# The last feed-forward chunk in halves of features, the next step's first transposes inside its last block, and the next weight piece converted in halves, its low half by GpSimd

## The reference

```python
def _rmsnorm(x, g):
    y = x * lax.rsqrt(jnp.mean(x * x, axis=-1, keepdims=True) + EPS)
    return y * g
def _swiglu(x, wg, wu, wd):                  # wg, wu: 1024 x 2816, wd: 2816 x 1024
    return (jax.nn.silu(x @ wg) * (x @ wu)) @ wd
# first block, per layer: feed-forward, mixer, feed-forward, each between two norms
h = _swiglu(_rmsnorm(x, g[0]), ...);  x = x + 0.5 * _rmsnorm(h, g[1])
h = mixer(_rmsnorm(x, g[2]), ...);    x = x + _rmsnorm(h, g[3])
h = _swiglu(_rmsnorm(x, g[4]), ...);  x = x + 0.5 * _rmsnorm(h, g[5])
# second block, per layer: no norm behind the net
h = h + mixer(rmsnorm(h, g_mix), ...)
h = h + swiglu(rmsnorm(h, g_ffn), ...)
```

## Time and profile before

| | |
|---|---|
| median of three executions | 1610.89 us |
| the profiled execution | 1613.06 us, of which span 1611.3 us |
| PE busy | 1577.4 us (98%), 9504 matmuls |
| PE weight loads | 1361.7 us (85%) |
| DVE busy | 1030.3 us (64%) |
| ACT busy | 800.1 us (50%) |
| POOL busy | 84.9 us (5%) |
| chain that ended last | PE 90%, DVE 5%, ACT 2%, issue 2%, POOL 1% |
| granted clock of PE | 0.996 on the mean |

### The profile page before, as it was taken

One profiled execution on the slowest core, in us unless ns is written; L12 is line 12 of the kernel. 1 busy time (PEld: TensorE's weight loads), 2 busy tenths in 40 slices (PEclk: granted clock), 3 DMA queues, 4 the chain that ended last, 5 costly groups with the idle time before them and its releaser, 6 DMA issues.

```text
span 1611.3 us, 24376 instructions
## 1 busy us (share of the span) xinstructions
PE 1577.4 (98%) x9504; PEld 1361.7 (85%) x9504; DVE 1030.3 (64%) x1172; ACT 800.1 (50%) x962; POOL 84.9 (5%) x125
## 2 busy tenths in 40 slices
PE   8999999999999999999999999989999999899998
PEld 6888887788898888889788888878888989788887
DVE  6566686656667666765566667666666665666665
ACT  5444555744446444554454446555444453554443
POOL 6000010000000000001200000000000000400000
PEclk9999999999999999999999999999999999999999
DMA  8555555365565565463365554536555655155652
GB/s 264 185 192 198 183 155 147 131 204 187 183 208 184 182 208 179 160 224 118 105 225 182 185 206 157 175 127 206 193 200 182 205 189 181 64 173 182 208 178 83
DMA packets 198248, 285.98 MB, mean 177 GB/s; under 512 B 9266, under 2 KB 149617, under 8 KB 198178
## 3 DMA queue, kind: packets, MB, share of 16 engines
q1 hardware_dynamic: 193152, 270.83, 50.4%
q0 software_dynamic: 4304, 13.38, 2.6%
q10 hardware_dynamic: 722, 0.79, 0.1%
HBM read 282.34 MB, written 1.05 MB: 176 GB/s over the span
## 4 chain that ended last, share of the span: by engine, by line
PE 90%; DVE 5%; ACT 2%; issue 2%; POOL 1%; DMA 0%; ACTq 0%; DVEq 0%; POOLq 0%
PE ps L1772 41%; PE ps L1945 22%; PE ps L1952 11%; PE ps L1762 5%; PE ps L1835 4%; DVE w_lo L1161 2%; PE ps L1792 1%; POOL shared L644 1%; PE ps L2178 1%; DVE xn L1350 1%; PE ps L2231 1%; PE ps L2134 1%; PE ps L1884 1%; PE ps L2258 1%; DMA raw<-in_ffn_w_up_dram 0%
## 5 line engine op out<-in xcount | busy, mean ns | idle before, releaser
L1161 DVE TENSOR_TENSOR w_lo<-raw,w_hi 128x2048 fp32r<-128x2048 f32 x254 | 580.3, 2290 | 330.9 <-ACT w_hi L750 330.8
L750 ACT CAST w_hi<-raw 128x2048 fp32r<-128x2048 f32 x256 | 487.6, 1905 | 104.2 <-PE ps L1772 44.8
L1945 PE MATMUL ps<-xt,w_hi 128*128 128x512 f32 x1536 | 365.1, 390 | 0.0
L1945 PEld LDWEIGHTS ps<-xt,w_hi 128*128 128x128 f32 x1536 | 285.3, 188 | 57.2
L1772 PE MATMUL ps<-xt,w_hi 128*128 128x256 f32 x1472 | 208.9, 284 | 0.9 <-DVE w_lo L1161 0.4
L1952 PEld LDWEIGHTS ps<-xt,w_lo 128*128 128x128 f32 x1536 | 196.9, 191 | 7.5
L1952 PE MATMUL ps<-xt,w_lo 128*128 128x256 f32 x1536 | 199.2, 283 | 0.0
L1772 PEld LDWEIGHTS ps<-xt,w_hi 128*128 128x128 f32 x1472 | 190.4, 192 | 4.8 <-DVE w_lo L1161 3.7
L1772 PE MATMUL ps<-w_hi,ht_hi 128*128 128x512 f32 x528 | 163.4, 391 | 0.0
L1772 PE MATMUL ps<-w_hi,ht_lo 128*128 128x512 f32 x528 | 163.0, 390 | 0.0
L1772 PE MATMUL ps<-w_lo,ht_hi 128*128 128x512 f32 x528 | 162.8, 389 | 0.0
(11 more groups left out here) (253 smaller groups left out, 1432.2 us busy)
## 6 DMA issues: line engine op xcount, KB each, us to landing
raw<-in_ffn_w_down_dram SPq DMA_DIRECT2D x132, 512.0 KB, 4.2
raw<-in_ffn_w_gate_dram SPq DMA_DIRECT2D x131, 512.0 KB, 3.7
raw<-in_ffn_w_up_dram SPq DMA_DIRECT2D x131, 512.0 KB, 4.7
raw<-in_fox_w_in_dram SPq DMA_DIRECT2D x24, 512.0 KB, 4.6
raw<-in_a_w_in_dram SPq DMA_DIRECT2D x24, 512.0 KB, 4.5
raw<-in_w_kv_dram SPq DMA_DIRECT2D x16, 512.0 KB, 5.1
raw<-in_ab_w_in_dram SPq DMA_DIRECT2D x14, 512.0 KB, 4.7
gain<-in_norm_g_dram POOLq DMA_DIRECT2D x11, 512.0 KB, 4.1
```

Of the source, the lines that this page charges most:

```text
L750: nc.scalar.copy(w_hi[slot][:, :], raw[slot][:, :]).then_inc(hi_made, 1)
L1161: nc.vector.tensor_tensor(w_lo[slot][:, :], raw[slot][:, :], w_hi[slot][:, :].bitcast(F32), ALU.subtract).then_inc(lo_made, 1)
L1945: nc.tensor.matmul(ps[:, GU_LOOP + b, :], w_hi[slot][:, col[b]], xt[:, kb, :], start=kb == 0, stop=False)
```

## The change

1. **Halves of features** (`last_gate_up`, `last_half`). The second piece of the last chunk's gate and up product is taken feature block by feature block: first gate and up of the first 128 features (bank 4), then of the second 128 (bank 5). All that DVE and ACT do to the chunk is done per half, on 128 x 256, with its own semaphores for the first half.
2. **Order of the last blocks.** The four blocks on tile 0 come first and the four on tile 1 behind them, so that four blocks instead of three stand behind `y_tile0`. The first block of chunk 10 waits for the first half only.
3. **Transposes inside.** The first quarter's transposes stand inside the net's last block, with three of its six matmuls behind them; and in the out steps of SWA and FOX inside the last product, as they did in those of MLSTM and REL (six matmuls behind them).
4. **The next piece in halves** (`border_hi`, `border_lo`). ACT rounds the first half of the columns behind the table's change and the second half behind tile 0's inverse root. The low part is made by POOL, in two subtractions of 128 x 1024, instead of by DVE in one of 128 x 2048. DVE waits for it only ahead of the next piece's low part.

```diff
-            s["early"] = s["to_ffn"] and bool(n) and steps[n - 1]["g"] is None
+            s["early"] = s["kind"] == "pre" and bool(n)
...
+        borders = [s["piece"] + s["n"] for s in steps if s["kind"] == "ffn" and s["piece"] + s["n"] < n_pieces]
...
+            def border_lo(p):                                   # POOL
+                slot = p % RING
+                pool.wait_ge(lo_made, p)
+                for part in range(2):
+                    cols = slice(part * PIECE // 2, (part + 1) * PIECE // 2)
+                    pool.wait_ge(*((hi_made, p + 1) if part else (border_hi_half, borders.index(p) + 1)))
+                    ins = nc.gpsimd.tensor_tensor(w_lo[slot][:, cols], raw[slot][:, cols],
+                                                  w_hi[slot][:, cols].bitcast(F32), ALU.subtract)
+                ins.then_inc(lo_made, 1)
...
                         post_square(post, 0)                    # ACT, norms
+                        if p in borders:
+                            border_hi(p, 1)
                         hi_upto(p + 1)
                         turn(s, 0)
                         post_square(post, 1)
...
-                chunk_(NC - 1, 0, pieces=False)                 # ACT, ffn
+                for k in range(2):
+                    act.wait_ge(*((gate_scaled, (NC - 1) * (f + 1)) if k else (gate_first_half, f + 1)))
+                    nc.scalar.activation(sg[:, k, :], sg[:, k, :], ACT.Silu)\
+                        .then_inc(silu_made if k else silu_first_half, 1)
+                    act.wait_ge(*((hid_made, (NC + 1) * (f + 1)) if k else (hid_first_half, f + 1)))
+                    nc.scalar.copy(ht_hi[0][:, k, :], hid[:, k, :]).then_inc(ht_hi_made if k else ht_hi_first_half, 1)
                 nc.scalar.preload_act_table_set(TABLES)
                 end = p + 3 * NC
-                hi_skip(end)
-                hi_upto(end)
+                if end in borders:
+                    border_hi(end, 0)
+                hi_skip(end + 1)
...
                 turn(s, 2, 3)                                   # DVE, norms
+                if p in borders:
+                    dve.wait_ge(lo_made, p + 1)
                 lo_upto(p + RING - 1)
...
-                chunk_(NC - 1, 0, pieces=False, banks=GU_LAST)  # DVE, ffn
-                end = p + 3 * NC
-                lo_skip(end)
-                lo_upto(end)
+                last_half(0)
+                last_half(1)
+                lo_skip(p + 3 * NC + 1)
...
-                gate_up(q - 2, banks=GU_LAST)                   # PE, ffn
+                last_gate_up(q - 2)
                 pe.wait_ge(ht_lo_made, f * NC + NC - 1)
                 split(q)
                 down_block(q, 0, 0, 1)
                 down_block(q, 1, 0, 1)
-                down_block(q, 0, 1, 1)
-                pe.wait_ge(ht_lo_made, f * NC + NC)
+                pe.wait_ge(ht_lo_first_half, f + 1)
                 split(q + 1)
                 down_block(q + 1, 0, 0, 0)
+                pe.wait_ge(ht_lo_made, f * NC + NC)
                 down_block(q + 1, 1, 0, 0, stop=True).then_inc(y_tile0, 1)
+                down_block(q, 0, 1, 1)
                 down_block(q, 1, 1, 1).then_inc(piece_used, 1)
                 down_block(q + 1, 0, 1, 0)
-                down_block(q + 1, 1, 1, 0, stop=True).then_inc(piece_used, 1)
+                pre = steps[steps.index(s) + 2]
+                down_block(q + 1, 1, 1, 0, stop=True,
+                           between=(lambda: turn(pre, 0)) if pre["kind"] == "pre" else None).then_inc(piece_used, 1)
```

69 lines of the change are left out of this document (57 added, 12 removed).

## The result

The changed kernel takes 1615.13 us (median of 7 runs, 1613.26 to 1617.57), the kernel before beside it 1611.12 (7 runs, 1610.38 to 1613.6). The ratio is 1.0022, 95% interval 1.0013 to 1.0031, so 2 to 5 us longer. The forecast was 1613.0 with a range of 1606.7 to 1615.8.

What follows compares the result with a forecast made beforehand. PE, busy 98%, was taken as the bound, with the start of tile 1's square setting the price at norm borders. Terms of +2.4, +1.2, -0.7 and -0.8 sum to +2.1: median 1613.0 us, range 1606.7 to 1615.8.

Steps and rivals of the forecast that it cites:

- What bounds the borders: At borders with a norm, the start of tile 1's square sets the price; PE's next product follows 13.28 us behind.
- Halves of the last chunk: In each net's last chunk, doubled DVE and ACT operations cost 0, with +3 us kept as an end.
- Rival 4: The halves of the last chunk stall PE 0.5 us in each net: 1616, chance 0.05.
- POOL's price: At the borders, one POOL subtraction of 1024 columns takes 2.35 us, with 2.54 as the other end.
- The exclusion: At norm borders DVE's multiplication waits for POOL's second subtraction; PE stands 1.55 us, tile 1's square starts at E + 2.13.
- rival 1: At the borders POOL's and DVE's subtractions do not exclude each other: sum -4.0 us, 1606.9, chance 0.15.
- Rival 2: At the borders POOL excludes DVE for part of its instruction only, judged from `alibi_b`: about -2 us, 1609, chance 0.13.
- the outs: Out steps of SWA and FOX: with transposes inside the product, tile 1's square starts 0.4 us earlier each, -0.8 in all.
- Sizes in the sum: Second to fourth border +2.4 us, first +1.2, fifth -0.7, out steps of SWA and FOX -0.8, net 5 0: sum +2.1.
- Rival 3: PE's stalls lower the clock to 1.2 GHz: 1614.7 if at the first border, 1619.8 at all four norm borders; chance 0.17.
- POOL's upper price: At the borders a POOL subtraction takes 2.54 us instead of 2.35, adding 4 x 0.19 to the range's upper end.
- same: Whole kernel's time within 0.2% (3.2 us) of the kernel before, between 1607.7 and 1614.1 us: chance 0.58.

Runs made afterwards that it cites:

- dve_low: Changed kernel with both low halves at the borders made by DVE ahead of the norm, POOL idle there: 1608.33 us, ratio 0.9983 to the kernel before.

## Why the prediction was right, and where it was off

- **What bounds the borders.** Right: the product came 13.28 behind the square of tile 1 in the changed kernel too.
- **Halves of the last chunk, 0.** Right, from both sides: PE stands nowhere in the last blocks with them, and 1.1 a net is lost without them in the new order. Rival 4 falls with this.
- **POOL's price, 2.35.** It was 2.39 to 2.41 when nothing held it, 2.73 when DVE's add did. The second began 0.48 ahead of the end of that add (489.06), where I had it begin behind it, and its end at 491.31 is E + 0.19 instead of E + 0.25 (E = 491.12, where the net would have ended without the stall).
- **The exclusion.** Right in kind and size: hold to 0.14 ahead of POOL's end (forecast 0.13), stall 1.47 (1.55), square at E + 2.18 (E + 2.13). The stall is 0.08 shorter than forecast, but the transposes take 0.41 and not 0.37 (491.91 to 492.32), and the first matmul behind them 0.32 and not 0.23 (492.32 to 492.64). Taking POOL away, cutting its instructions and lengthening them moved the time as the exclusion says, and a POOL instruction without any tie in data did the same. Rivals 1 and 2 fall. Rival 2's evidence was weak for two reasons: it came from one-input instructions, and of the eight `alibi_b` operations, put at 1.17 to 1.23, two took 1.43, one of them beside the DVE subtraction that lasted 984 ns. What rival 1 would have brought is about what dve_low shows, -3.2 and not -4.0: 0.1 less at each of three borders, 0.2 at the first, 0.3 at the outs.
- **Sizes in the sum.** Second to fourth border +2.6 instead of +2.4, first +1.33 instead of +1.2, fifth -0.7 as forecast. The outs brought 0.5 instead of 0.8: there the product starts 1.89 behind the transposes (304.66 - 302.77) and not 0.37 + 1.36 = 1.73, for the most part by the same two costs, and ACT's square (304.86) follows it. Sum +2.7.
- **The clock.** The rest of the measured difference, +4.0 and +5.2 in two sets whose intervals begin at 2.1 and 3.1, is not at a place of the table. In the runs beside the experiments the changed kernel had a mean granted clock of 0.9954 and the kernel before 0.9975. Within the kernel before a run was 1.1 us longer for each 0.001 (27 runs), within the experiments' other kernels 0.7 to 1.0, and within the changed kernel 1.8 (10 runs). The 0.0021 between the kernels would so be 1.5 to 3.8 us, and could fill the gap of 2.5 in that set. It is a correlation. The 0.0021 may also count too much: in the profiles 0.0004 of it stands behind the last matmul, where the changed kernel has 4.5 us at 1.2 GHz on the mean and the kernel before 3.1, and where PE has nothing to lose. Rival 3 named a fall behind the first border; the profiles have it once in four, and in that profile stretches elsewhere are missing in exchange. So rival 3 is not shown to cost anything on the whole, and why the timed runs differ by more than 2.7 us stays open.

The mechanism was right, and the located places carry 2.7 of the 4.0 us. That the number came out inside the range had luck in it: the forecast's median was 2 us low, and the same kernel measured again took 1615.99 us, 0.2 above the range's end. The step that was thin was one of judgement. I had named four things that could each only lengthen the time (the clock, POOL's upper price, more at each border, less gained at the outs), and still put "same" at 0.58 and "slower" at 0.27. The outcome lay above the bound of 0.2%, on the slower side.

## What to carry to other kernels

Work handed to GpSimd is not free because GpSimd is idle: if its instruction reads two SBUF inputs, a DVE instruction with two SBUF inputs waits for its end (0.14 us short of it here). So look at what DVE has on the critical path in that stretch, and cut GpSimd's instructions short, or leave the work to an idle stretch of DVE. By the count, 256 columns gave back 5.4 of the 5.9 us that taking the work away from GpSimd gave. Where one matmul in thousands waits, count the same matmul through both traces; it showed 0.24 us that 11 runs could not.

## What was not expected of the hardware

- A POOL multiplication with one SBUF input of 1024 columns lasted 3.27 us, longer than the two-input subtraction (2.87) that also began 0.05 behind DVE's add, and held DVE for 0.65 only.
- The hold works both ways: POOL's subtraction grew from 2.40 to 2.73, 2.85 and 2.87 when it began beside a DVE instruction with two SBUF inputs.
- A stall of 3.5 us ahead of the transposes came with 1.2 GHz four times in four, and in three of them the clock fell before the stall was over; one of 1.3 us was followed by it once in sixteen.
